# ScalarE's weight splits between the steps of a block, the last delta set's norm inside the output blocks, and the low part first in the merge, in a ten-stage float32 kernel

## The chip, the core and the metric

The kernel runs on one core of a Trainium2 chip. The metric is the time of the whole program on the device in microseconds (us). Five engines work side by side: TensorE (PE, matmuls; PEld is its weight load), VectorE (DVE), ScalarE (ACT), GpSimd (POOL) and SyncE (SP, which issues most DMAs). They meet through semaphores.

## What is computed

The reference passes one sequence of 256 tokens with 1024 features through ten residual stages, all in float32:

```python
def first_block(x, ...):                       # twice (DEPTH = 2)
    h = rms_norm(x, attn_norm[l]);  x = x + hybrid_mixer(h, ...)   # three attentions, merged
    h = rms_norm(x, ffn_norm[l]);   x = x + conv_ffn(h, ...)
# hybrid_mixer ends in
    z = g_a * (o_moba @ w_branch_moba) + g_b * (o_nsa @ w_branch_nsa) + g_c * (o_gla @ w_branch_gla)
    return z @ w_out
# conv_ffn
    a = causal_depthwise_conv(a, 3 taps) + conv_b;  return (gelu(a) * g) @ w_down
def second_block(x, ...):                      # twice
    ff = swiglu(rms_norm(h));   h = h + 0.5 * rms_norm(ff)
    mix = short_conv_mixer or gated_deltanet_mixer;  h = h + rms_norm(mix)
    ff = swiglu(rms_norm(h));   h = h + 0.5 * rms_norm(ff)
# gated_deltanet_mixer ends in
    o = o * rsqrt(mean(o * o) + eps) * norm_w        # per head, 16 heads of 128
    o = o * silu(z);  return o @ w_out
```

## The kernel before

**Stages.** In order: HYBRID, FFN1, HYBRID, FFN1, FFN2, SHORT, FFN2, FFN2, DELTA, FFN2. HYBRID is the three-branch mixer, FFN1 the convolving feed-forward layer, FFN2 the Silu-gated one, SHORT the short convolution, DELTA the gated delta rule. A stage ends in blocks, one for each tile of 128 hidden features: 22 in an FFN stage, 8 in HYBRID and SHORT, 16 in DELTA.

**Weights and their halves.** Weights come as panels of 128 x 1024 floats (512 KB), loaded by SP into a ring of six slots (`raw`). A float32 product is made of three faster ones: ScalarE writes the high part of a panel, `hi(p)` (L982 to L988: it waits until the panel has landed and the product that used the slot six panels ago is done), VectorE the low part, `lo(p)` (L1513 to L1516: raw minus high part), and TensorE takes high x high, high x low and low x high (`mm3`, L2275 to L2277). SP reloads a slot when the `lo` of its panel is done. `hi_to(p)` and `lo_to(p)` do all that is left up to panel p.

**A block f.** TensorE makes the up products (two panels of 24 matmuls of 256 columns in an FFN stage; one in HYBRID, `branches`, which takes the three branch weights) and then `down(f - 2)`: 12 matmuls of 512 columns with the hidden tile of block f - 2 as weights, added up in four banks over all blocks. In between, VectorE reads the up products (`first`, `second`), ScalarE applies Silu, or in FFN1 the middle tap (L1046) and, after VectorE's two other taps (L1652, L1655), Gelu (L1050); VectorE multiplies to `h`; ScalarE writes its high part `hhi` (L1059, which waits for `down(f - 2)`, the last user of that buffer), VectorE its low part `hlo` (`h_low`, L1676), one block later. `down(f)` needs `hlo` of f and the `lo` of its own panel. The panels of a stage lie in the order of use, and `ahead_panel(s, f)` is the last panel that block f + 1 needs (in DELTA the down panel of block f).

**Order on the engines.** Each engine's order is written by hand and is kept: an instruction that waits holds all that stands behind it. ScalarE's body of block f is: the `hi` of what block f + 1 needs, then `ffn_block(s, f)`. VectorE's is: the `lo` of what block f + 1 needs, then its own `ffn_block`. In FFN stages blocks 4 to 19 run in a hardware loop of two blocks a turn (`run_blocks`); the others are written out. In HYBRID ScalarE is one block further ahead than elsewhere. There VectorE's block is five merge steps (three products with the gates, two sums, L1617 to L1624) and then `h_low(f - 1)`.

**DELTA.** 32 tiles of q, k and v and 15 of 16 z products run in 47 slots t = 0 to 46. The delta rule is worked off in four sets of four heads, on a schedule by slot. A set's outputs are copied by ScalarE, squared and summed over each head's columns (`delta_o_squared`, eight squares, L1415), scaled and shifted by VectorE (`delta_o_added`), rooted by ScalarE (`delta_o_root`, needs a load of its function table), inverted and multiplied in by VectorE (`delta_o_inv`, `delta_o_scaled`). For the last set the squares and the sum stand in slot 46, the root behind output block 1, inverse and scaling behind block 2. An output block f: TensorE transposes head f's output (2 matmuls, L2371; it waits for `h` of f - 2, and heads 12 to 15, pairs 6 and 7, for the last set's scaling), in block 1 it also makes the sixteenth z product, and then `down(f - 2)`. VectorE makes `h` (L1667).

Of the kernel before, what the change touches and what calls it, by code (L numbers as in the profile page):

```python
# [39 lines left out]
SET = 2 * KSET  # L40
SETS = KH // KSET
# [259 lines left out]
def build(nc, stages, arrays):  # L301
# [14 lines left out]
    with ExitStack() as ctx:  # L316
# [661 lines left out]
        def _(act):  # L978
# [53 lines left out]
            def ffn_block(s, f, turn):  # L1032
# [7 lines left out]
                elif kind in (FFN2, DELTA):  # L1040
                    act.activation(act_out[:, sl, :], first[:, sl, 2:], ACT.Silu).then_inc(act_done, 1)  # L1041
                elif kind != HYBRID:

                    c = plus(convs_before(s) + f, turn, UNROLL)
                    if kind == FFN1:
                        act.activation(conv[:, sl, :], first[:, sl, 2:], ACT.Identity,  # L1046
                                       scale=tap(s, 2, f, turn), bias=conv_bias(s, f, turn)) \
                            .then_inc(tap_done, 1)
                        act.wait_ge(conv_done, c + 1)
# [9 lines left out]
                act.activation(hhi[:, sl, :], h[:, sl, :], ACT.Copy).then_inc(hhi_done, 1)  # L1059

            def blocks_of(s):
                def body(f, turn):
                    nb = n_blocks(s)
                    if turn is not None:
                        for j in range(n_up(s) + 1):
                            hi(up_panel(s, f + 1, j), turn)
                        split[0] = up_panel(s, nb - 2, n_up(s)) + 1
                    else:
                        hi_to(ahead_panel(s, f + 1 if stages[s][0] == HYBRID and 0 < f < nb - 1 else f))
                    ffn_block(s, f, turn)  # L1070
                    if f == 1 and stages[s][0] == DELTA:
                        delta_o_root(1)
                    if f == nb - 1:
                        hi_to(down_panel(s, f) + LEAD)
                run_blocks(act, s, body)
# [332 lines left out]
            def delta_o_squared(n):  # L1408

                act.wait_ge(d["o_copied"], 2 * (n + 1))  # L1410
                for i in range(SET * CHUNKS):
# [13 lines left out]
            def delta_step(s, n, o):  # L1425
# [17 lines left out]
                if p == 22:  # L1443
                    delta_o_squared(n)
# [57 lines left out]
        def _(dve):  # L1502
# [95 lines left out]
            def ffn_block(s, f, turn):  # L1598
# [13 lines left out]
                elif kind == HYBRID:  # L1612

                    dve.wait_ge(y["merged"], 3 * KT * (hybrids_before(s) + 1))
# [10 lines left out]
                    if f >= 1:  # L1625
                        h_low(s, f - 1, turn)
# [13 lines left out]
                else:  # L1640
                    dve.tensor_tensor(first[:, sl, 2:], pair[:, 0:S], rstd[:], ALU.mult).then_inc(gate_scaled, 1)  # L1641
                    dve.tensor_tensor(second[:, sl, :], pair[:, S:], rstd[:], ALU.mult).then_inc(pair_read, 1)

# [35 lines left out]
            def blocks_of(s):  # L1679
                def body(f, turn):  # L1680
                    nb = n_blocks(s)
                    if turn is not None:
                        for j in range(n_up(s) + 1):
                            lo(up_panel(s, f + 1, j), turn)
                        split[0] = up_panel(s, nb - 2, n_up(s)) + 1
                    else:
                        lo_to(ahead_panel(s, f))
                    ffn_block(s, f, turn)
                    if f == 2 and stages[s][0] == DELTA:
# [512 lines left out]
            def delta_step(s, n, o):  # L2202
# [23 lines left out]
                if p == (23 if n + 1 < SETS else 22):  # L2226
                    delta_o_added(n)
# [721 lines left out]
```

## Time and profile before

| | us |
|---|---|
| median of 3 runs | 2023.91 (2023.28 to 2025.52) |
| the profiled execution | 2025.12 |
| its span, first to last instruction | 2023.3 |
| TensorE busy | 1979.2 |
| VectorE busy | 1389.5 |
| ScalarE busy | 1105.3 |
| mean granted TensorE clock | 0.995 |

The page has the busy time of each engine; the timeline lists instructions with start, duration and, in brackets, the idle time of their engine before them with what ended it. A matmul's duration covers more than the time for which it holds the engine, so successive matmuls overlap and the distance of their starts is what counts.

### The profile page before, as it was taken

What the parts mean: (1) busy time and instruction counts of PE and PEld (TensorE: products, weight loads), DVE (VectorE), ACT (ScalarE), POOL (GpSimd) and SP (SyncE); (2) the same over time, 40 slices, a digit from 0 to 9 for tenths busy, and PEclk for the clock granted to TensorE, in tenths of its full rate; (3) what the DMA queues carried; (4) which work ended last, traced back from release to release, by engine and by line L of the source; (5) the groups of instructions that cost most, each with busy time, mean ns of one, the idle gap of its engine ahead of it and who ended that gap; (6) DMA issues with size and microseconds to landing.
All of it is one profiled execution on the core that took longest, in us unless ns stands there. A gap on an engine that the chain in (4) does not pass through costs nothing. (4 is left out here: it accounts for less than half of the span.)

```text
span 2023.3 us, 40582 instructions
## 1 busy us (share of the span) xinstructions
PE 1979.2 (98%) x15118; PEld 1841.5 (91%) x15118; DVE 1389.5 (69%) x2352; ACT 1105.3 (55%) x1836; POOL 125.4 (6%) x204
## 2 busy tenths in 40 slices
PE   8999999999999999999999999999999999999998
PEld 6999899989998999899999999999999999979997
DVE  5687877676788777765567765575559876567555
ACT  5665555566654655554454544464448786546443
POOL 2031000000130000000000000000002422000000
PEclk9999999999999999999999999999999999999999
DMA  9433655554335555465546455555555444345552
GB/s 309 146 126 126 210 193 187 191 178 146 133 119 177 178 187 187 167 208 187 188 166 212 154 195 187 187 178 187 188 178 166 134 140 149 126 146 186 187 188 93
DMA packets 117812, 348.42 MB, mean 172 GB/s; under 512 B 23288, under 2 KB 35912, under 8 KB 117184
## 3 DMA queue, kind: packets, MB, share of 16 engines
q1 hardware_dynamic: 114960, 335.23, 48.9%
q0 software_dynamic: 2736, 11.59, 1.8%
q8 instruction: 80, 1.31, 0.3%
q14 instruction: 36, 0.29, 0.0%
HBM read 340.81 MB, written 5.96 MB: 171 GB/s over the span
## 5 line engine op out<-in xcount | busy, mean ns | idle before, releaser
L1516 DVE TENSOR_TENSOR wlo<-raw,whi 128x1024 fp32r<-128x1024 f32 x621 | 737.9, 1229 | 382.6 <-ACT whi L988 381.5
L2275 PE MATMUL bank<-xhi,whi 128*128 128x256 f32 x3368 | 955.5, 284 | 9.7 <-DVE xlo L1527 5.2
L2276 PE MATMUL bank<-xlo,whi 128*128 128x256 f32 x3368 | 941.7, 280 | 0.0
L2277 PE MATMUL bank<-xhi,wlo 128*128 128x256 f32 x3368 | 941.1, 279 | 0.0
L2275 PEld LDWEIGHTS bank<-xhi,whi 128*128 128x128 f32 x3368 | 633.8, 188 | 25.2 <-issue 7.3
L2276 PEld LDWEIGHTS bank<-xlo,whi 128*128 128x128 f32 x3368 | 634.2, 188 | 5.7
L2277 PEld LDWEIGHTS bank<-xhi,wlo 128*128 128x128 f32 x3368 | 633.6, 188 | 0.0
L988 ACT ACTIVATE whi<-raw 128x1024 fp32r<-128x1024 f32 x621 | 621.2, 1047 | 6.8 <-PE bank L2277 5.3
L2275 PE MATMUL bank<-whi,hhi 128*128 128x512 f32 x688 | 273.7, 398 | 6.5 <-DVE hlo L1676 5.1
L2277 PE MATMUL bank<-whi,hlo 128*128 128x512 f32 x688 | 271.6, 395 | 0.0
L2276 PE MATMUL bank<-wlo,hhi 128*128 128x512 f32 x688 | 271.1, 394 | 0.0
L1059 ACT ACTIVATE hhi<-h 128x256 fp32r<-128x256 f32 x172 | 72.1, 419 | 266.7 <-PE bank L2277 182.6
L1041 ACT ACTIVATE act_out<-first 128x256 f32<-128x256 f32 x89 | 37.4, 420 | 230.7 <-DVE first L1641 230.3
L2275 PEld LDWEIGHTS bank<-whi,hhi 128*128 128x128 f32 x688 | 129.5, 188 | 34.8 <-issue 10.5
L2277 PEld LDWEIGHTS bank<-whi,hlo 128*128 128x128 f32 x688 | 129.8, 189 | 30.2
L2276 PEld LDWEIGHTS bank<-wlo,hhi 128*128 128x128 f32 x688 | 130.4, 190 | 23.3
L1641 DVE TENSOR_TENSOR first<-bank,rstd 128x256 f32<-128x256 f32 x132 | 55.8, 422 | 52.8 <-PE bank L2277 52.6
L1676 DVE TENSOR_TENSOR hlo<-h,hhi 128x256 fp32r<-128x256 f32 x172 | 71.8, 417 | 12.6 <-ACT hhi L1059 12.6
L1046 ACT ACTIVATE conv<-first,cols 128x256 f32<-128x256 f32 x44 | 26.5, 603 | 92.9 <-DVE first L1641 92.9
L1670 DVE TENSOR_TENSOR h<-act_out,second 128x256 f32<-128x256 f32 x132 | 55.8, 422 | 22.7 <-ACT act_out L1050 21.6
L1141 ACT ACTIVATE arena<-arena 128x256 f32<-128x256 f32 x48 | 20.0, 418 | 70.2 <-DVE arena L1791 70.2
L929 POOL DMA_DIRECT2D arena<-gains_in x6 | 3.3, 553 | 865.8 <-DVE arena L1555 734.8
(367 smaller groups left out, 1792.6 us busy)
## 6 DMA issues: line engine op xcount, KB each, us to landing
raw<-panels SPq DMA_DIRECT2D x621, 512.0 KB, 4.3
arena<-w_in POOLq DMA_DIRECT2D x2, 2048.0 KB, 10.0
arena<-relay SPq DMA_DIRECT2D x8, 512.0 KB, 4.8
arena<-gains_in POOLq DMA_DIRECT2D x6, 512.0 KB, 4.0
relay<-arena POOLq DMA_DIRECT2D x4, 512.0 KB, 8.1
relay<-arena SPq DMA_DIRECT2D x4, 512.0 KB, 4.1
x<-x_in SPq DMA_DIRECT2D x1, 1024.0 KB, 5.0
arena<-bias_table POOLq DMA_DIRECT2D x8, 128.0 KB, 4.6
```

What stands on the lines that cost most here:

```text
L988: act.activation(whi[slot][:], raw[slot][:], ACT.Copy).then_inc(hi_done, 1)
L1041: act.activation(act_out[:, sl, :], first[:, sl, 2:], ACT.Silu).then_inc(act_done, 1)
L1046: act.activation(conv[:, sl, :], first[:, sl, 2:], ACT.Identity, scale=tap(s, 2, f, turn), bias=conv_bias(s, f, turn)) \
L1059: act.activation(hhi[:, sl, :], h[:, sl, :], ACT.Copy).then_inc(hhi_done, 1)
L1141: act.activation(g, g, ACT.Tanh, scale=0.5).then_inc(y["merged"], 1)
L1516: dve.tensor_tensor(wlo[slot][:], raw[slot][:], whi[slot][:].bitcast(F32), ALU.subtract) \
L1641: dve.tensor_tensor(first[:, sl, 2:], pair[:, 0:S], rstd[:], ALU.mult).then_inc(gate_scaled, 1)
L1670: dve.tensor_tensor(h[:, sl, :], gated, second[:, sl, :], ALU.mult).then_inc(h_done, 1)
L1676: dve.tensor_tensor(hlo[:, sl, :], h[:, sl, :], hhi[:, sl, :].bitcast(F32), ALU.subtract) \
L2275: pe.matmul(dst, w_hi, a_hi, start=start, stop=False, skip_group_check=True)
L2276: pe.matmul(dst, w_hi, a_lo, start=False, stop=False, skip_group_check=True)
L2277: return pe.matmul(dst, w_lo, a_hi, start=False, stop=stop, skip_group_check=True)
```

## The change

Three edits in the order of work; no arithmetic is altered.

In FFN stages ScalarE takes the weight splits for block f + 2 (`ahead`) inside block f: one right after its Silu or tap, the rest after `hhi`. Before, they stood at the start of block f + 1's body. VectorE, in block 0 of FFN stages, does one `lo` fewer ahead of reading the first products, and that one after. In DELTA's blocks from 1 on ScalarE is one down panel further ahead. The last set's eight squares move from slot 46 to behind `hhi` of blocks 1 and 2, four each; the sum goes from slot 46 to behind VectorE's block 3, the root behind ScalarE's block 3, inverse and scaling behind VectorE's block 5. In HYBRID's blocks VectorE makes `hlo` of block f - 1 before the merge steps of f instead of after.

```diff
@@ ScalarE, ffn_block
-            def ffn_block(s, f, turn):
+            def ffn_block(s, f, turn, ahead):
...
                 elif kind in (FFN2, DELTA):
                     act.activation(act_out[:, sl, :], first[:, sl, 2:], ACT.Silu).then_inc(act_done, 1)
+                    for p in ahead[0:1]:
+                        hi(p, turn)
...
                             .then_inc(tap_done, 1)
+                        for p in ahead[0:1]:
+                            hi(p, turn)
                         act.wait_ge(conv_done, c + 1)
...
                 act.activation(hhi[:, sl, :], h[:, sl, :], ACT.Copy).then_inc(hhi_done, 1)
+                for p in ahead[1:]:
+                    hi(p, turn)
@@ ScalarE, blocks_of
                     if turn is not None:
-                        for j in range(n_up(s) + 1):
-                            hi(up_panel(s, f + 1, j), turn)
-                        split[0] = up_panel(s, nb - 2, n_up(s)) + 1
+                        ahead = [up_panel(s, f + 2, j) for j in range(n_up(s) + 1)]
+                        split[0] = up_panel(s, nb - 1, n_up(s)) + 1
+                    elif loops(s):
+                        hi_to(ahead_panel(s, f))
+                        ahead = list(range(split[0], ahead_panel(s, f + 1) + 1)) if f < nb - 1 else []
+                        split[0] += len(ahead)
                     else:
-                        hi_to(ahead_panel(s, f + 1 if stages[s][0] == HYBRID and 0 < f < nb - 1 else f))
-                    ffn_block(s, f, turn)
-                    if f == 1 and stages[s][0] == DELTA:
-                        delta_o_root(1)
+                        hi_to(ahead_panel(s, f + 1 if stages[s][0] in (HYBRID, DELTA) and 0 < f < nb - 1 else f))
+                        ahead = []
+                    ffn_block(s, f, turn, ahead)
+                    if stages[s][0] == DELTA:
+                        if f in (1, 2):
+                            delta_o_squared(SETS - 1, range(4 * f - 4, 4 * f))
+                        if f == 3:
+                            delta_o_root(1)
@@ ScalarE, delta_step
-                if p == 22:
-                    delta_o_squared(n)
+                if p == 22 and n + 1 < SETS:
+                    delta_o_squared(n, range(SET * CHUNKS))
@@ VectorE, ffn_block
                 elif kind == HYBRID:
 
+                    if f >= 1:
+                        h_low(s, f - 1, turn)
                     dve.wait_ge(y["merged"], 3 * KT * (hybrids_before(s) + 1))
...
                     dve.tensor_tensor(h[:, sl, :], second[:, sl, :], conv[:, sl, :], ALU.add).then_inc(h_done, 1)
-                    if f >= 1:
-                        h_low(s, f - 1, turn)
                     return
...
                     dve.tensor_tensor(second[:, sl, :], pair[:, S:], rstd[:], ALU.mult).then_inc(pair_read, 1)
+                    if f == 0:
+                        lo_to(ahead_panel(s, f))
@@ VectorE, blocks_of
+                    elif loops(s) and f == 0:
+
+                        lo_to(ahead_panel(s, f) - 1)
                     else:
                         lo_to(ahead_panel(s, f))
                     ffn_block(s, f, turn)
-                    if f == 2 and stages[s][0] == DELTA:
+                    if f == 3 and stages[s][0] == DELTA:
+                        delta_o_added(SETS - 1)
+                    if f == 5 and stages[s][0] == DELTA:
                         delta_o_inv(1)
                         delta_o_scaled((6, 7))
@@ VectorE, delta_step
-                if p == (23 if n + 1 < SETS else 22):
+                if p == 23 and n + 1 < SETS:
                     delta_o_added(n)
```

## Rows read from the trace of the kernel before

**Rows 1.** The page: span, busy time, the weight copy, and loads until landing.
```profile
span 2023.3 us, 40582 instructions
...
PE 1979.2 (98%) x15118; PEld 1841.5 (91%) x15118; DVE 1389.5 (69%) x2352; ACT 1105.3 (55%) x1836; POOL 125.4 (6%) x204
...
L988 ACT ACTIVATE whi<-raw 128x1024 fp32r<-128x1024 f32 x621 | 621.2, 1047 | 6.8 <-PE bank L2277 5.3
...
raw<-panels SPq DMA_DIRECT2D x621, 512.0 KB, 4.3
```

**Rows 2.** Timeline (start, us, engine, what, idle before), FFN1's loop: PE, then ACT.
```profile
332.79 0.28 PE L2275 MATMUL bank<-xhi,whi 128*128 128x256 f32 x1
...
338.39 0.39 PE L2275 MATMUL bank<-whi,hhi 128*128 128x512 f32 x1
...
341.17 0.28 PE L2275 MATMUL bank<-xhi,whi 128*128 128x256 f32 x1
...
336.24 0.42 ACT L1050 ACTIVATE act_out<-conv 128x256 f32<-128x256 f32 x1 [1.29 <-DVE conv L1655]
...
337.55 2.94 ACT L988 ACTIVATE whi<-raw 128x1024 fp32r<-128x1024 f32 x3
```

**Rows 3.** Stretches: length, busy us (count) of PE, PEld, DVE, ACT, POOL; clock, DMA.
```profile
350.00:375.00 25.00, 25.00 (x181) 23.44 (x180) 17.67 (x28) 12.97 (x18) 0.00 (x0) 1.00 0.57 189
...
1767.98:1772.40 4.42, 4.41 (x12) 3.42 (x13) 1.47 (x3) 2.86 (x4) 0.00 (x0) 0.61 0.28 106
...
1776.29:1813.59 37.30, 35.70 (x155) 27.05 (x155) 21.52 (x34) 15.05 (x22) 0.00 (x0) 1.00 0.45 155
```

**Rows 4.** Timeline, first HYBRID stage, its block 1 on DVE and down(0) on PE.
```profile
203.09 0.41 DVE L1617 SCALAR_TENSOR_TENSOR second<-arena,bank 128x256 f32<-128x256 f32 x1
...
204.88 0.42 DVE L1676 TENSOR_TENSOR hlo<-h,hhi 128x256 fp32r<-128x256 f32 x1
205.21 2.35 DVE L1516 TENSOR_TENSOR wlo<-raw,whi 128x1024 fp32r<-128x1024 f32 x2
...
205.44 0.47 PE L2275 MATMUL bank<-whi,hhi 128*128 128x512 f32 x1 [1.71 <-DVE hlo L1676]
```

**Rows 5.** Timeline, first FFN1 stage, end of DVE's block 1 and PE's block 3.
```profile
262.38 0.42 DVE L1670 TENSOR_TENSOR h<-act_out,second 128x256 f32<-128x256 f32 x1 [0.48 <-ACT act_out L1050]
264.23 3.50 DVE L1516 TENSOR_TENSOR wlo<-raw,whi 128x1024 fp32r<-128x1024 f32 x3 [1.43 <-ACT whi L988]
...
265.60 0.36 PE L2275 MATMUL bank<-xhi,whi 128*128 128x256 f32 x1 [1.03 <-DVE wlo L1516]
```

**Rows 6.** Timeline, DELTA's output blocks: PE, DVE and ACT, then the last blocks.
```profile
1761.71 0.60 PE L2371 MATMUL bank<-masks,arena 128*128 128x128 f32 x4
1762.07 0.36 PE L2275 MATMUL bank<-xhi,whi 128*128 128x256 f32 x1
...
1765.17 0.24 DVE L2181 SCALAR_TENSOR_TENSOR arena<-arena 128x4 f32<-128x4 f32 x2 [2.83 <-ACT psq L1415]
...
1766.45 0.48 DVE L1667 SCALAR_TENSOR_TENSOR h<-bank,cols,arena 128x256 f32<-128x256 f32 x1
...
1767.08 0.41 PE L2371 MATMUL bank<-masks,arena 128*128 128x128 f32 x2 [1.96 <-DVE h L1667]
...
1768.71 1.28 ACT L1423 ACT_TABLE_LOAD   x1
...
1776.58 0.42 ACT L1059 ACTIVATE hhi<-h 128x256 fp32r<-128x256 f32 x1 [2.02 <-DVE h L1667]
...
1777.98 1.23 DVE L1516 TENSOR_TENSOR wlo<-raw,whi 128x1024 fp32r<-128x1024 f32 x1 [1.44 <-ACT whi L988]
1779.12 0.42 DVE L1676 TENSOR_TENSOR hlo<-h,hhi 128x256 fp32r<-128x256 f32 x1
...
1779.68 0.47 PE L2275 MATMUL bank<-whi,hhi 128*128 128x512 f32 x1
...
1817.31 0.47 PE L2275 MATMUL bank<-whi,hhi 128*128 128x512 f32 x1 [0.69 <-DVE hlo L1676]
```

More of the change, by code:

```diff
@@ L1406, in delta_o_copied, with delta_o_squared @@
                     act.activation(o_pair(KSET * n + g), bank[g][:], ACT.Copy).then_inc(d["o_copied"], 1)
-            def delta_o_squared(n):
+            def delta_o_squared(n, parts):
                 act.wait_ge(d["o_copied"], 2 * (n + 1))
-                for i in range(SET * CHUNKS):
+                for i in parts:
                     at = SET * CHUNKS * n + i
```

## The prediction

> **What bounds the kernel now.** I read the page first: over a span of 2023.3 us TensorE is busy 1979.2 us, VectorE 69%, ScalarE 55% [rows 1]. That alone says little, because the ends of matmuls are modelled, so I looked at the starts. In the loop of an FFN stage 48 matmuls of 256 columns go from 332.79 to 338.39 (0.117 us each) and 12 of 512 columns from there to 341.17 (0.232 us each); a block is 8.38 us, without a hole [rows 2]. A stretch of such a loop is busy 25.00 of 25 us at full clock [rows 3]. Here a faster ScalarE or VectorE buys nothing. So the change can pay only where a matmul starts later than the one before it allows. I went through TensorE's timeline for such starts and asked of each what ended the wait, and then through the DELTA output blocks, whose holes are so short and regular that no row calls them idle.
>
> The true hole is the idle time that a row gives plus the overlap of the matmul before it (its duration less its spacing: 0.28 - 0.12, or 0.39 - 0.23, 0.16 us in both [rows 2]).
>
> **Part 1, the merge's low part first.** In block 2 of a HYBRID stage TensorE starts down(0) at 205.44 after 1.71 idle, so the hole is 1.87 us and TensorE was free at 203.57. It waits for hlo(0), which VectorE makes at 204.88 behind the five merge steps that began at 203.09, although hhi(0) was made in the block before [rows 4]. Moved to the front, hlo(0) runs 203.09 to 203.50 and down(0) starts at about 203.65, with the 0.14 that now lies between hlo's end (205.30) and the matmul. The five merge steps slide back by 0.33, but VectorE's sum over the block is the same, so the two lo steps still begin at 205.21, the first ending at about 206.43 (half of 2.35 us for two). TensorE, 1.79 us earlier, is done with down(0) at 203.65 + 2.78 = 206.43 and waits again for that lo, some 0.14. Behind it VectorE has nothing late: its next lo pair is one block of work on (2.35 + 2.1 = 4.4 us, so from 209.6), and wanted at 212.1. I take 1.65 us per stage, bounds 1.3 and 1.8; the other HYBRID stage has the same hole (its row, not shown, says 1.71 idle as well). Sum 3.3 us. The new order queues hlo(f-1)'s wait for hhi ahead of the merges; hhi(f-1) is ScalarE's first act after h(f-1), before its weight copies, so nothing is held.
>
> **Part 2, weight copies between steps, FFN stages.** The body of block f+1 followed at once on that of block f, so three hi copies already ran right behind hhi(f). What moves is one of them, to between the tap (or Silu) of f and hhi(f). In the loop ScalarE idles 1.29 us there, waiting for VectorE's convolution before the Gelu [rows 2]; a copy takes 1.05 [rows 1], and 0.95 when one follows another (2.94 for three) [rows 2]. It fits, at no cost, and the two behind hhi end 0.95 sooner. If the cover were gone, each block would put about 1 us on a cycle of ScalarE and VectorE that the copies leave 1 us shorter: zero again. In the loop this is worth nothing, for TensorE has no hole. Worth something is the start of FFN1: at 265.60 TensorE waits for the first lo of a group of three that began at 264.23 after ScalarE's copies; idle 1.03, hole 1.2 [rows 5]. After the change that panel's hi is made right after the tap of block 1, some 3 us before VectorE asks for it, so VectorE can begin this lo once it has made h (262.80, [rows 5]) instead of at 264.23, 1.4 us earlier, and block 0 gains another half microsecond because only two lo's stand before its scaling. TensorE is free at 264.40, the lo would end near 262.8 to 264.0: the hole goes, 1.2 us, bounds 0.9 and 1.2, twice (the second FFN1 stage has the like, idle 1.04). Sum 2.4 us. The four FFN2 stages' starts show no wait for wlo, I cost them at nothing.
>
> **Part 3, the last DELTA set's norm, and the copies one block ahead.** Four holes stand in the output blocks [rows 6].
> (a) Before block 2's transposes TensorE idles 1.96, hole 2.12: h(0) is made at 1766.45, behind a lo, behind VectorE's wait of 2.83 us for ScalarE's eight squares. down(0) follows at 1768.0 [rows 3]. Without squares and sum in front, VectorE does that lo straight after its read of the last z product, which TensorE had finished by 1761.71, so at about 1762.3 to 1763.5; h(0) ends at 1763.9, hhi(0) at 1764.4, hlo(0) at 1764.8. TensorE ends the last up product at 1767.08 - 2.12 = 1764.96, transposes, and starts down(0) at about 1765.2: 2.8 us, bounds 2.6 and 2.8.
> (b) down(0) itself runs at a granted clock of 0.61, between the levels 1.2 and 2.4 GHz [rows 3]: 4.42 us instead of 2.78, right behind that idle time; 1.6 us, if the clock stays as full as it is behind this stretch; bounds 0 and 1.6.
> (c) Then downs that start 3.39 us apart (37.30 us for eleven from 1776.29 to 1813.59 [rows 3]). They are not TensorE's: VectorE waits 1.44 us in each for a hi, ScalarE 2.02 for h. The cycle is hi 1.05, lo 1.15, hlo 0.33, h 0.48, hhi 0.32 with short waits between, and hlo's end releases TensorE. With hi one panel ahead VectorE's share is lo, hlo, h = 2.0 us and ScalarE's hhi, hi = 1.4; the cycle is cut, TensorE's own work sets the pace: 12 x 0.232 = 2.78 and two transposes. Transposes that wait for nothing take 0.36 for four (1761.71 to 1762.07), so 0.18 for two; the blocks now show 0.52. I take 3.04 us a block, bounds 2.96 and 3.15. From down(1) to down(13) there are 12 intervals, and the restart ahead of down(1) is shorter too, by 0.3: 12 x 0.35 + 0.3 = 4.5 us, bounds 3.0 and 5.4. The load of a panel, 4.3 us to landing [rows 1], is issued six panels ahead, some 18 us.
> (d) Before down(14), at 1817.31, TensorE idles 0.69, hole 0.85: hlo(14) stands behind a lo that waited for its hi. With hi and lo early this goes: 0.8 us, bounds 0.6 and 0.9.
> What is moved in: squares of 1.2 us on ScalarE in each of blocks 1 and 2, a root with table load of 1.5 us in block 3, sum and 1.5 us of inverse and scaling on VectorE in blocks 3 and 5. ScalarE has 3.04 - 1.3 = 1.7 us free in a block and VectorE 1.0, and both run one to two blocks ahead of TensorE; the scaled pairs are wanted in block 12. I cost them at 0, bounds 0 and 0.8 loss. Sum 2.8 + 1.6 + 4.5 + 0.8 = 9.7.
>
> A rule weighed here: before the root the row shows a load of 1.28 us at 1768.71 and the root at once behind it, with no further pause [rows 6]. The Trainium skill, "ScalarE: Activation LUTs", section "What ACT_TABLE_LOAD costs", adds a drain of about 1.4 us to each switch. By that figure ScalarE would lose 2.9 instead of 1.5 us in block 3, still inside its lead; the sum is the same.
>
> **Sum.** 3.3 + 2.4 + 9.7 = 15.4 us. Made against the profiled execution, 2023.3 span and 2025.1 in all, it gives 2009.7 [rows 1]; this execution lies 1.2 above the median of the three runs (2023.9), so the time I give is 2023.9 - 15.4 = 2008.5. The bounds of the parts add to 9.8 to 16.7 us, so 2007.2 to 2014.1, and the runs of before spread over 2.2 us.
>
> **Rivals.**
> A. The DELTA blocks stay near 3.39 us, because something else paces them: for instance TensorE's restart behind the two transposes (0.52 now, though no row of it names a wait). For it: the first matmul after them is stretched (0.47 against 0.40). Against it: hlo ends just 0.14 before each restart (1779.54, 1779.68 [rows 6]) and both engines wait on each other with no slack. Gain 15.4 - 4.5 = 10.9, 2013.0.
> B. The clock falls elsewhere or still falls in down(0), with 1.6 to 2 us lost: 2010.3. For it: such drops stand where TensorE has idled. Against it: 12 blocks each with a pause ran at 1.00 [rows 3].
> C. Slower. The moved copy waits in ScalarE's queue for its panel, and Gelu, hhi and all copies wait behind it, where before hhi went first. The load of a panel of block f+2 is issued when the lo of block f is done, before TensorE's 332.79 [rows 2]; it is now asked for at the tap's end, which is 336.24 - 1.29 + 8.38 = 343.3 in the next block, so landing must take over 10.5 us against a median of 4.3 [rows 1]. If it took half a microsecond more than that, each of 132 FFN blocks could pay up to it: 132 x 0.5 = 66, 2074.
> D. Nothing changes: ScalarE's order was not what held VectorE, and each hole returns behind the next wait (for the lo of down(1), for hhi behind the end of the last down): within 4 us, about 2022. The releasers named in the rows speak against it in all five places.
>
> **Chances.** Forecast 0.70, A 0.13, B 0.09, C 0.03, D 0.05. What a measurement can tell from no change is 0.2%, 4 us. Faster 0.92, the same 0.05, slower 0.03. The range takes in the bounds, A and B and half the spread of runs: 2005.5 to 2014.5.
>
> **What would show it.** After: no idle before down(0) of the HYBRID stages over 0.3 us; no wait for wlo in block 3 of FFN1; block 2's transposes of DELTA directly behind the last up product, full clock in down(0), starts of downs 3.0 to 3.1 us apart, no ACT row with an idle of 2.02 for h; FFN loops still 8.38 us. Wrong I would be if downs stand 3.3 or more apart, if a wait for hhi or for a landed panel appears in their place, or if a FFN loop's block grows.

## The result, and the profile after

The changed kernel takes 2004.03 us (median of 4 runs, 2003.44 to 2004.42). The kernel before, run beside it on the same chip, takes 2024.59 us (2023.28 to 2025.52). The ratio is 0.9899, with a 95% interval of 0.9882 to 0.9916: 20.6 us faster, where 15.4 was forecast. The time lies 1.5 us below the range. The sign and most of the sum were right, and something of about 5 us was missing from it.

The page of the changed kernel (span; busy time; groups of instructions with busy time, mean ns of one, and idle time of the engine before them; a load's median until landing) stands against [rows 1]:

```profile
span 2002.0 us, 40567 instructions
...
PE 1970.4 (98%) x15118; PEld 1838.6 (92%) x15118; DVE 1401.1 (70%) x2352; ACT 1100.3 (55%) x1836; POOL 125.7 (6%) x204
...
L1529 DVE TENSOR_TENSOR wlo<-raw,whi 128x1024 fp32r<-128x1024 f32 x621 | 749.6, 1230 | 218.1 <-ACT whi L988 215.1
...
L988 ACT ACTIVATE whi<-raw 128x1024 fp32r<-128x1024 f32 x621 | 632.3, 1045 | 7.0 <-PE bank L2297 5.5
L2295 PE MATMUL bank<-whi,hhi 128*128 128x512 f32 x688 | 272.7, 396 | 0.0
...
raw<-panels SPq DMA_DIRECT2D x621, 512.0 KB, 3.6
```

The span is 21.3 us shorter. No engine does less: the copies and low parts have the counts of before, and TensorE's busy time fell by 8.8 us only. What went is waiting. Down projections have no idle time ahead of them (0.0), and VectorE waits 215 us for ScalarE's weight copies. In the kernel before, the same two groups read:

```profile
L1516 DVE TENSOR_TENSOR wlo<-raw,whi 128x1024 fp32r<-128x1024 f32 x621 | 737.9, 1229 | 382.6 <-ACT whi L988 381.5
...
L2275 PE MATMUL bank<-whi,hhi 128*128 128x512 f32 x688 | 273.7, 398 | 6.5 <-DVE hlo L1676 5.1
```

A fall of 166 us in VectorE's wait and a gain of 21: most of that wait never reached TensorE. To find where the 21 us came from I took the start of each matmul in both timelines (both kernels issue the same 15118 in the same order) and read how the difference, after less before, moves along the run:

| stretch, by the time in the kernel before | difference at its start and end | gained | forecast |
|---|---|---|---|
| HYBRID 1, to 212.0 | +0.06, -1.60 | 1.7 | 1.65 |
| start of FFN1 stage 1, 240 to 280 | -1.60, -3.07 | 1.5 | 1.2 |
| **end of FFN1 stage 1, 400 to 450** | -3.07, -4.62 | 1.5 | **0** |
| HYBRID 2, to 628 | -4.62, -6.29 | 1.7 | 1.65 |
| start of FFN1 stage 2, 670 to 690 | -6.32, -7.78 | 1.5 | 1.2 |
| **end of FFN1 stage 2, 840 to 870** | -7.78, -9.32 | 1.5 | **0** |
| up to the middle of DELTA, 870 to 1570 | -9.32, -9.39 | 0.1 | 0 |
| **middle of DELTA, 1570 to 1592** | -9.39, -10.79 | 1.4 | **0** |
| DELTA output blocks, 1760 to 1830 | -10.78, -21.31 | 10.5 | 9.7 |

Timeline, first HYBRID stage of the changed kernel (start, us, engine, what), against [rows 4]:

```profile
203.13 0.42 DVE L1691 TENSOR_TENSOR hlo<-h,hhi 128x256 fp32r<-128x256 f32 x1
...
203.69 0.47 PE L2295 MATMUL bank<-whi,hhi 128*128 128x512 f32 x1
...
205.25 2.35 DVE L1529 TENSOR_TENSOR wlo<-raw,whi 128x1024 fp32r<-128x1024 f32 x2
...
206.62 0.36 PE L2295 MATMUL bank<-xhi,whi 128*128 128x256 f32 x1
```

hlo runs first, and down(0) starts at 203.69 (forecast 203.65), 1.81 us earlier. Some 0.15 of it is given back ahead of the up product at 206.62, which follows 0.28 behind a matmul instead of 0.23 and has a longer duration: the pause for the lo pair at 205.25.

Timeline, first FFN1 stage, VectorE's block 1 and TensorE's block 3, against [rows 5]:

```profile
259.79 1.22 DVE L1529 TENSOR_TENSOR wlo<-raw,whi 128x1024 fp32r<-128x1024 f32 x1
261.31 2.36 DVE L1529 TENSOR_TENSOR wlo<-raw,whi 128x1024 fp32r<-128x1024 f32 x2 [0.30 <-ACT whi L988]
...
262.63 0.28 PE L2295 MATMUL bank<-xhi,whi 128*128 128x256 f32 x1
```

The lo that TensorE used to wait for is made right behind h, and TensorE goes on at 262.63 without an idle time.

Timeline, DELTA's output blocks, against [rows 6]; below it two stretches (length, busy us and count of PE, PEld, DVE, ACT, POOL, granted clock, DMA share, GB/s), against [rows 3]:

```profile
1754.18 0.38 PE L2391 MATMUL bank<-masks,arena 128*128 128x128 f32 x2
1754.31 0.47 PE L2295 MATMUL bank<-whi,hhi 128*128 128x512 f32 x1
...
1760.89 1.28 ACT L1436 ACT_TABLE_LOAD   x1
1762.18 0.21 ACT L1436 ACTIVATE arena<-arena 128x8 f32<-128x8 f32 x1
...
1766.35 0.48 PE L2295 MATMUL bank<-whi,hhi 128*128 128x512 f32 x1
...
1769.37 0.48 PE L2295 MATMUL bank<-whi,hhi 128*128 128x512 f32 x1
...
1772.49 0.42 ACT L1063 ACTIVATE hhi<-h 128x256 fp32r<-128x256 f32 x1 [1.63 <-PE bank L2297]
1772.94 0.43 DVE L1691 TENSOR_TENSOR hlo<-h,hhi 128x256 fp32r<-128x256 f32 x1 [0.82 <-ACT hhi L1063]
```

```profile
350.00:375.00 25.00, 25.00 (x181) 23.44 (x180) 17.90 (x28) 12.86 (x18) 0.00 (x0) 1.00 0.53 185
...
1754.31:1757.31 3.00, 3.00 (x17) 2.43 (x16) 2.35 (x5) 2.65 (x11) 0.00 (x0) 1.00 0.51 178
```

The transposes follow the last up product, down(0) runs at a granted clock of 1.00, downs start 3.02 us apart in the two rows (1766.35, 1769.37) and 3.01 in the mean, and ScalarE's hhi waits for the end of a down product on TensorE, no longer for h. VectorE waits 0.82 us for hhi, which the prediction had named as a sign of being wrong, but TensorE has no idle row in any of these blocks: it sets the pace here now. The FFN loop is what it was, busy 25.00 of 25 us.

### The profile page after: what moved, and what is told of

Its sections match the earlier page's. It is cut to its first block, busy times and chain, and to the rows that moved or that the text cites. A ratio compares the mean times of both kernels' runs of the same rounds, so it can differ in the third digit from the quotient of the medians.

```text
span 2002.0 us, 40567 instructions
## 1 busy us (share of the span) xinstructions
PE 1970.4 (98%) x15118; PEld 1838.6 (92%) x15118; DVE 1401.1 (70%) x2352; ACT 1100.3 (55%) x1836; POOL 125.7 (6%) x204
## 4 chain that ended last, share of the span: by engine, by line
PE 90%; DVE 4%; ACT 3%; issue 1%; DMA 1%; POOL 1%; SPq 0%; DVEq 0%; ACTq 0%; POOLq 0%
PE bank L2295 28%; PE bank L2296 27%; PE bank L2297 27%; PE bank L2774 1%; ACT whi L988 1%; PE bank L2585 1%; DVE wlo L1529 1%; DVE arena L1568 1%; PE bank L2329 1%; PE bank L2558 0%; DVE conv L2030 0%; PE bank L2546 0%; PE bank L2338 0%; DVE xlo L1540 0%; DMA relay<-arena 0%
## 5 line engine op out<-in xcount | busy, mean ns | idle before, releaser
L1529 DVE TENSOR_TENSOR wlo<-raw,whi 128x1024 fp32r<-128x1024 f32 x621 | 749.6, 1230 | 218.1 <-ACT whi L988 215.1
L988 ACT ACTIVATE whi<-raw 128x1024 fp32r<-128x1024 f32 x621 | 632.3, 1045 | 7.0 <-PE bank L2297 5.5
```

Source lines behind the costliest of these rows:

```text
L988: act.activation(whi[slot][:], raw[slot][:], ACT.Copy).then_inc(hi_done, 1)
L1529: dve.tensor_tensor(wlo[slot][:], raw[slot][:], whi[slot][:].bitcast(F32), ALU.subtract) \
```

## The experiments

"Before" is the kernel before, run beside each on the same chip (medians 2025.15 to 2025.66); shifts are differences of matmul starts, as in the table above, from one profile of each kernel. The medians also take in differences in stretches that no edit touches, as in the middle of DELTA below: e4 gains 7.9 us by its median and 5.9 by the shifts where its edit acts, e5 2.2 and 3.1. So what a part is worth is read from the shifts. Line numbers differ a little from kernel to kernel.

### The parts, each alone

**e1**: the merge's low part first, nothing else.

```diff
                 elif kind == HYBRID:
+                    if f >= 1:
+                        h_low(s, f - 1, turn)
...
                     dve.tensor_tensor(h[:, sl, :], second[:, sl, :], conv[:, sl, :], ALU.add).then_inc(h_done, 1)
-                    if f >= 1:
-                        h_low(s, f - 1, turn)
```

> The kernel before with the low part first in the merge and nothing else. Theory (separate holes): both HYBRID stages lose 1.65 us, 3.3 in all, and the first FFN1 stage still has its wait for wlo of 1.2 us at its block 3 and for x of 1.2 us behind its last product. Rival (the parts help each other, the change is worth more than its parts): under 2 us alone. Rival (the merge part frees VectorE for the whole stage): over 5 us.

Measured: 2021.88 us against 2025.47, 0.9983 (0.9974 to 0.9993). The HYBRID stages gain 1.67 and 1.68 us, 3.35 together, and starts and ends of FFN1 stand as they were.

**e2**: all of the DELTA hunks and nothing else (copies one block ahead, the squares in blocks 1 and 2, root in 3, sum in 3, scaling in 5).

```diff
-                        hi_to(ahead_panel(s, f + 1 if stages[s][0] == HYBRID and 0 < f < nb - 1 else f))
+                        hi_to(ahead_panel(s, f + 1 if stages[s][0] in (HYBRID, DELTA) and 0 < f < nb - 1 else f))
...
+                        if f in (1, 2):
+                            delta_o_squared(SETS - 1, range(4 * f - 4, 4 * f))
+                        if f == 3:
+                            delta_o_root(1)
```

> The kernel before with both edits of DELTA's output blocks (copies one panel further ahead, norm of the last set moved) and nothing else. Theory: 10.5 us faster, starts of successive downs 3.02 us apart, down(0) at full clock. Rival (the granted clock in the middle of DELTA depends on the change): 11.5 to 12 us, with one spell of low clock less there in every run; if that spell is chance, the run lands at 10.5 or at 11.8 according to its own trace.

Measured: 2014.75 against 2025.47, 0.9949 (0.9932 to 0.9966). Output blocks: 10.7 us.

**e3**: all of the FFN hunks and nothing else (`ahead` between tap or Silu and hhi, in start, loop and end; block 0's lo moved).

```diff
+                        for p in ahead[0:1]:
+                            hi(p, turn)
                         act.wait_ge(conv_done, c + 1)
...
+                for p in ahead[1:]:
+                    hi(p, turn)
```

> The kernel before with the edits of the FFN stages alone (copies between the steps, one lo after the first read). Theory (lag): 2 x (1.2 to 1.3 at the start + 1.5 to 1.6 at the end of FFN1) = 5.6 us faster; the wait for x behind the last product of FFN1 is gone. My prediction had only the start: 2.4 us.

Measured: 2018.41 against 2025.47, 0.9968 (0.9958 to 0.9978). Each FFN1 stage gains 1.4 us at its start and 1.55 at its end. The gains of e1, e2 and e3 by medians (3.6, 10.7, 7.1) add to 21.4, against 20.6 for the whole change. By the shifts where the edits act they are 3.35, 10.7 and 5.9, 19.95 in all, against 19.9 in the whole change (21.3 less the 1.4 in the middle of DELTA): the three parts are independent. So the end of FFN1 was what the forecast lacked, and it comes from the FFN edit.

### Why does an edit of copies help the end of FFN1?

In the kernel before, the last matmuls of a FFN1 stage and VectorE's work beside them read so:

```profile
424.01 0.42 DVE L1641 TENSOR_TENSOR first<-bank,rstd 128x256 f32<-128x256 f32 x1
...
428.55 2.36 DVE L1516 TENSOR_TENSOR wlo<-raw,whi 128x1024 fp32r<-128x1024 f32 x2 [0.52 <-ACT whi L988]
430.83 2.48 DVE L1579 TENSOR_TENSOR x<-x,bank 128x512 f32<-128x512 f32 x4
...
432.25 1.93 PE L2318 MATMUL bank<-masks,x 128*128 128x128 f32 x13 [1.04 <-DVE x L1579]
```

and in the changed kernel:

```profile
419.39 0.42 DVE L1654 TENSOR_TENSOR first<-bank,rstd 128x256 f32<-128x256 f32 x1 [2.56 <-PE bank L2297]
...
423.94 2.36 DVE L1529 TENSOR_TENSOR wlo<-raw,whi 128x1024 fp32r<-128x1024 f32 x2 [0.52 <-ACT whi L988]
426.22 2.47 DVE L1592 TENSOR_TENSOR x<-x,bank 128x512 f32<-128x512 f32 x4
...
427.64 2.26 PE L2338 MATMUL bank<-masks,x 128*128 128x128 f32 x16
```

The transposes of x at the stage's end wait for VectorE's update of x, which stands behind two lo's, behind h, behind the last block's first read. That hole makes 1.1 of the 1.55; the other 0.4 are short pauses before the last two downs (425.24 and 428.17 in the kernel before), each 0.14 behind the end of an hlo that is as late. Before, VectorE reached that first read without an idle time, so it was late. After, it had waited 2.56 us for TensorE. One theory was that the copies between steps in the loop make each block's cycle shorter and so work the delay off. The rival was that the delay is made once, at the stage's start, and only carried. Three kernels part them.

**e4**: copies between steps in blocks 0 to 2 only, with block 0's lo moved; loop and end as before (the line is shown against the changed kernel's; the loop has the order of before).

```diff
-                        ahead = list(range(split[0], ahead_panel(s, f + 1) + 1)) if f < nb - 1 else []
+                        ahead = list(range(split[0], ahead_panel(s, f + 1) + 1)) if f < 3 else []
```

> As the FFN edits alone, but only in blocks 0, 1 and 2; the loop and the end are those of before. Theory L (the lag of VectorE behind TensorE that the start leaves is carried through the loop, since the cycle of ScalarE and VectorE there is as long as TensorE's block, and shows at the end): the start's hole goes and the lag in the loop shrinks by 1 to 2 us, so that the end's hole shrinks too, 4.5 to 5.6 us in all. Rival E (the end's hole is made by the order of the last two blocks alone): 2.4 to 2.6 us, hole at the end as before, 1.1 us each.

Measured: 2017.57 against 2025.47, 0.9963 (0.9949 to 0.9977). Starts 1.4 and 1.4, ends 1.57 and 1.54: all that e3 gives, with the loop of before.

**e5**: the opposite, block 3, the loop and block 20 without the start, lo not moved.

```diff
+                        ahead = list(range(split[0], ahead_panel(s, f + 1) + 1)) if f == 3 or nb - 2 <= f < nb - 1 else []
```

> The kernel before with copies between the steps in the loop and the last two blocks of the FFN stages, blocks 0 to 2 as before. Theory L: the holes at the start stay (1.2 us in each FFN1 stage), the cycle of ScalarE and VectorE is 1 us shorter in the loop, so VectorE's lag of 3.8 us behind the up products is gone after some four or five turns and the end's hole with it: 2 x 1.5 = 3.0 us faster. If the start's hole is also the cause of the end's hole directly: no gain.

Measured: 2022.92 against 2025.16, 0.9988 (0.9979 to 0.9998). Starts 0, ends 1.57 and 1.54.

**e6**: block 20, the last but one, alone; loop as before.

```diff
+                        ahead = list(range(split[0], ahead_panel(s, f + 1) + 1)) if nb - 2 <= f < nb - 1 else []
```

> As before, with a copy between the steps only in block 20, the last but one, of the FFN stages. Theory L: the lag in the loop stays at 3.8 to 3.4 us; in the last block VectorE's first read comes 1.0 us earlier (one copy less stands behind hhi), so the end's hole shrinks by about 1 us: 2 x 1.0 = 2 us faster, starts unchanged. If the lag of the loop fixes the end whatever stands there: no gain.

Measured: 2022.40 against 2025.16, 0.9988 (0.9979 to 0.9998). Starts 0, ends 1.19 and 1.25; what is left is the row at 430.62 below.

Each closes the hole at the end, e6 nearly, so it has more than one remedy. How each does it is seen in the middle of the loop. Each pair is TensorE's start of down, which is where the up products are done, and VectorE's first read of them: before (its down start is 338.39, [rows 2]), after, e4, e5. The row behind these is the end of the stage in e6.

```profile
342.04 0.42 DVE L1641 TENSOR_TENSOR first<-bank,rstd 128x256 f32<-128x256 f32 x1
```

```profile
343.71 0.39 PE L2295 MATMUL bank<-whi,hhi 128*128 128x512 f32 x1
343.92 0.42 DVE L1654 TENSOR_TENSOR first<-bank,rstd 128x256 f32<-128x256 f32 x1 [1.13 <-PE bank L2297]
```

```profile
345.12 0.39 PE L2292 MATMUL bank<-whi,hhi 128*128 128x512 f32 x1
346.59 0.42 DVE L1653 TENSOR_TENSOR first<-bank,rstd 128x256 f32<-128x256 f32 x1
```

```profile
346.43 0.39 PE L2285 MATMUL bank<-whi,hhi 128*128 128x512 f32 x1
346.63 0.42 DVE L1651 TENSOR_TENSOR first<-bank,rstd 128x256 f32<-128x256 f32 x1 [1.13 <-PE bank L2287]
```

```profile
430.62 2.26 PE L2330 MATMUL bank<-masks,x 128*128 128x128 f32 x16 [0.30 <-DVE x L1591]
```

VectorE's lag behind TensorE is 3.65 us before, 0.21 after, 1.47 in e4 and 0.20 in e5. Followed over blocks 2 to 21 of the stage, the lag goes

- before: 6.03, 4.31, 3.87, 3.82, ... 3.39, 3.31, 1.75;
- after: 3.74, 2.17, 0.59, 0.20, and 0.20 to the end;
- e4: 3.74, 2.15, 1.70, 1.64, ... 1.17, 1.07, 0.20;
- e5: 6.03, 4.31, 2.72, 1.54, 0.31, 0.20, and 0.20 to the end.

Before, the lag falls by some 0.03 us a block (3.82 in block 5, 3.39 in block 19): the cycle of ScalarE and VectorE takes that much less than TensorE's block of 8.38. Made in the first two blocks, it is still there 20 blocks later, and nothing shows it in between, because TensorE has its weights in time all the way. It comes due where the stage ends and TensorE wants x itself. Both theories hold a part: the start makes the lag and curing it there is enough (e4); the loop with copies between steps has more slack and works it off in three blocks (e5). Done together they don't add. Over both stages e4 gives 2.8 us at the starts and 3.1 at the ends, e5 gives the same 3.1 at the ends, and e3, which has both, gives 5.9.

**e11 and e12** split e4: only block 0's lo behind the first reads, and only the copies of the first blocks.

```diff
+                    if f == 0:
+                        lo_to(ahead_panel(s, f))
```

> The kernel before with VectorE's lo moved behind the first read in block 0 of FFN stages and nothing else. Theory: reads come 1.1 us earlier, but Gelu's table load sits behind the tap, so h gains 0.5 to 1 us; the hole at block 3 shrinks by as much and so does the end's: 2 x (0.5 to 1.0) x 2 holes = 2 to 4 us faster.

> The kernel before with the copies between the steps in blocks 0, 1 and 2 of the FFN stages, without the move of the lo. Theory: hi of block 3's first panel is ready early, so its lo follows h directly: 1.4 us at block 3, enough for the hole of 1.2; lag in the loop 1.6 to 2.2 us instead of 3.8; the end's hole almost gone: 2 x (1.2 + 1.0 to 1.5) = 4.4 to 5.4 us faster.

Measured: e11 2023.15 against 2025.66, 0.9992 (0.9982 to 1.0001): starts 0.67 and 0.71, ends nothing, 1.4 us in all, where its expectation had 2 to 4. Its lag is 5.52 in block 2, but from block 3 on it is that of before (4.30, 3.86): the lo move takes half a microsecond off one block, and the next wait takes it back. e12 2020.33, 0.9974 (0.9964 to 0.9984): starts 1.43 and 1.48, ends 1.12 and 1.07. The copies alone do the whole of the start, and lo and copies together the whole of the end.

**e9**: the changed kernel with two copies between tap and Gelu, to see how deep the cover is.

```diff
                             .then_inc(tap_done, 1)
-                        for p in ahead[0:1]:
+                        for p in ahead[0:2]:
                             hi(p, turn)
...
-                for p in ahead[1:]:
+                for p in ahead[2 if kind == FFN1 else 1:]:
```

> The changed kernel with two copies instead of one between FFN1's tap and its Gelu. The idle time there is 1.2 us, two copies take 2.0, so Gelu, h and hhi come 0.8 us later in each of 44 blocks and one copy less stands behind hhi. Theory (TensorE alone sets the pace of the loop; VectorE has lost its lag and waits for it): the same time as the changed kernel, FFN block 8.39 us. Rival (the room is used up and each block pays): 44 x 0.8 = 35 us slower.

Measured: 2004.85 against 2025.66, 0.9899 (0.9883 to 0.9916). Each start and end gains within 0.13 us of what it does in the changed kernel, and the loop's blocks are the same. VectorE's lag goes 4.42, 3.09, 1.71, 0.50, 0.20: worked off one block later. ScalarE has the room for a second copy, but it pays nothing.

### The DELTA blocks: are the two edits one?

**e7**: only the copies one block ahead. **e8**: only the norm moved into the blocks. Each is its share of e2's diff, the first hunk (`in (HYBRID, DELTA)`) and the rest.

> The kernel before with ScalarE one down panel further ahead in DELTA's blocks, the norm of the last set left in slot 46. Theory: starts of downs 3.02 us apart, last hole gone: 4.5 + 0.8 + 0.2 = 5.5 us faster, the idle time of 2.12 before block 2 and the low clock in down(0) stay. Rival: the copy of down(3) now stands ahead of hhi(2) and behind the root's table load, so hlo(1) or hlo(2) comes late: 4 us.

> The kernel before with only the norm of the last set moved into blocks 1 to 5. Theory: the idle time before block 2 (2.8 us to the start of down(0)) and the low clock (1.6 us) go: 4.4 us. Against it stands that the squares and the root lengthen a cycle that has no slack: 1.2 us in each of blocks 1 and 2, 1.5 in block 3: at worst 3.9 us back, so between 0.5 and 4.4 us faster. Together with the other edit this must give 10.1 to 10.5.

Measured: e7 2018.40 against 2025.16, 0.9965 (0.9953 to 0.9976), output blocks 6.1 us. e8 2024.93, 0.9994 (0.9984 to 1.0004), output blocks 0.8 us. The interval of e8 takes in 1, so only its shift tells. Together (e2) they give 10.7, so 3.8 us belong to neither alone. e8's timeline gives one reason: down(1) to down(4) on PE, then the lo's on DVE between them:

```profile
1770.52 0.47 PE L2280 MATMUL bank<-whi,hhi 128*128 128x512 f32 x1 [1.14 <-DVE hlo L1679]
1775.08 0.47 PE L2280 MATMUL bank<-whi,hhi 128*128 128x512 f32 x1 [1.32 <-DVE hlo L1679]
1779.98 0.47 PE L2280 MATMUL bank<-whi,hhi 128*128 128x512 f32 x1 [1.66 <-DVE hlo L1679]
1783.37 0.47 PE L2280 MATMUL bank<-whi,hhi 128*128 128x512 f32 x1 [0.15 <-DVE hlo L1679]
...
1773.37 1.22 DVE L1519 TENSOR_TENSOR wlo<-raw,whi 128x1024 fp32r<-128x1024 f32 x1 [2.60 <-ACT whi L988]
1778.28 1.23 DVE L1519 TENSOR_TENSOR wlo<-raw,whi 128x1024 fp32r<-128x1024 f32 x1 [2.81 <-ACT whi L988]
1781.66 1.23 DVE L1519 TENSOR_TENSOR wlo<-raw,whi 128x1024 fp32r<-128x1024 f32 x1 [1.43 <-ACT whi L988]
```

At down(1) e8 has gained 3.4 us. Then the squares (1.17 us on ScalarE, from 1771.12) and the root with its load (1.40 us, from 1775.80) stand in ScalarE's queue ahead of the copy that VectorE waits for (2.60 and 2.81 us, against 1.43 without them), in a cycle without slack. The next three intervals are 4.56, 4.90 and 3.39 us: 1.17 and 1.51 over the third, so 2.7 us are given back. In the changed kernel the same squares and root lie in the same blocks, and the downs are 3.01 apart. e7 shows the other side:

```profile
1768.03 0.41 PE L2371 MATMUL bank<-masks,arena 128*128 128x128 f32 x2 [1.96 <-DVE h L1667]
1768.94 0.47 PE L2275 MATMUL bank<-whi,hhi 128*128 128x512 f32 x1 [0.50 <-DVE hlo L1676]
```

The entry is as in [rows 6], with its idle time and a down(0) of 4.4 us, and behind it blocks of 3.01 in the mean. Here the low clock costs time: down(0) to down(1) takes 4.56 us, and hlo(1) had been ready for 2.6. In the kernel before it cost nothing. Whether the clock falls behind the same 1.96 us of idle time is not set by the code here: of the nine kernels that keep this entry, it fell in three (before, e4, e7) and stayed full in six (e1, e3, e5, e6, e11, e12). This is down(1) in the kernel before, then down(0) as a stretch and down(1) in e1, which has DELTA's code of before:

```profile
1772.90 0.48 PE L2275 MATMUL bank<-whi,hhi 128*128 128x512 f32 x1
```

```profile
1762.46:1765.24 2.78, 2.77 (x12) 2.30 (x13) 0.26 (x1) 2.46 (x4) 0.00 (x0) 1.00 0.41 167
```

```profile
1767.38 0.47 PE L2275 MATMUL bank<-whi,hhi 128*128 128x512 f32 x1 [1.68 <-DVE hlo L1676]
```

At a full clock down(0) takes 2.78 us instead of 4.42, and TensorE then waits 1.68 for hlo(1): from down(0) to down(1) it is 4.91 us in both, and in the other five kernels too. hlo(1) sets the start of down(1), and it comes earlier only with the copies ahead: down(1) gains 0.5 more than down(0) in e8, 1.9 in e2. So of the 3.8 us, some 1.56 (4.56 less 3.00) are the low clock that e7's profile happened to have, and the rest is the 2.7 that e8 gives back, less the 0.5 that both edits bring at down(1).

### The middle of DELTA: 1.4 us that no edit made

At 1583.44 of the kernel before, TensorE has idled 3 us for a transfer; the changed kernel has the same wait, untouched by any hunk. The timeline's row with its idle time, and the stretch of 7 us from there (columns as above), before:

```profile
1583.44 2.89 PE L2754 MATMUL bank<-arena 128*128 128x128 f32 x16 [3.14 <-DMA arena<-relay]
```

```profile
1583.44:1590.44 7.00, 6.50 (x34) 6.45 (x35) 5.30 (x13) 4.38 (x8) 0.00 (x0) 0.57 1.03 350
```

after:

```profile
1573.95 2.29 PE L2774 MATMUL bank<-arena 128*128 128x128 f32 x9 [3.04 <-DMA arena<-relay]
```

```profile
1573.95:1580.95 7.00, 6.26 (x42) 6.20 (x43) 6.06 (x14) 4.48 (x8) 0.00 (x0) 0.79 1.04 347
```

The granted clock of the same work behind the same idle time was 0.57 before and 0.79 after. These are means: the clock is at 1.00 or 0.50 (2.4 or 1.2 GHz), and the mean tells for how much of the stretch it was low. If the change does that, it should repeat; if chance does, another run of the same kernel shows another value; and if TensorE's idle time is the cause, matmuls put there should keep the clock at 1.00. **e15** is the changed kernel again. **e13** puts 13 matmuls of 512 columns in the wait, into a PSUM bank that nobody reads then (added work whose result is overwritten), **e14** 6 of them. **e10**, earlier, put 12 ahead of the wait for the transfer but behind another.

```diff
             def delta_w16(n):
+                if n == 0:
+                    pe.wait_ge(d["exponent"], 2 * KSET)
+                    pe.wait_ge(d["eg"], 2 * KSET)
+                    for _ in range(13):
+                        pe.matmul(bank[7][:], xhi[:, 0, 0:P], xhi[:, 0:2, :].rearrange("p a b -> p (a b)"),
+                                  start=True, stop=True, skip_group_check=True)
                 pe.wait_ge(d["tri_in"], 16 * (n + 1))
```

> The changed kernel with 12 matmuls of 512 columns, 2.8 us, whose result is overwritten, put where TensorE waits 3.2 us in the middle of DELTA for a DMA (before the first set's inverse is used). Theory (the spell of low clock right behind that wait follows from TensorE's idling, and costs 1.4 us for each of its two lengths): the spell is gone and the kernel 0.5 to 2 us faster, its runs closer together. Rival (the spell comes whatever TensorE did): same time or up to 1 us slower.

> The changed kernel with 13 matmuls of 512 columns (3.0 us, result overwritten) that start at once where TensorE waits 3.2 us in the middle of DELTA for a DMA. Theory (TensorE's idling brings the spell of low clock, which in the traces so far lasts 3.4, 6.8 or 10.2 us and costs 1.7, 2.6 or more): no spell there, 1.7 us or more faster than the changed kernel beside it. Rival (the spell comes from what follows, the small products of the inverse, which leave the engine little to do): the spell is there as before, same time.

> The same with 6 matmuls, 1.4 us, so that a hole of 1.8 us stays. Theory: no spell or a shorter one, 0 to 1.7 us faster than the changed kernel. Rival as above: same time as the changed kernel.

> The changed kernel itself, on the same chip as the two with the filled hole. Its spell in the middle of DELTA lasts 3.4, 6.8 or 10.2 us by chance; the gain against the kernel before on this chip is 20.5 to 21.5 us, and the mean of the middle spell is no shorter than before the change.

Measured: e10 2004.37 against 2025.66, 0.9898 (0.9881 to 0.9915). Its matmuls waited too: they start at 1573.14, after 2.17 us of idle time put down to ScalarE, so this kernel says nothing on the question. Then, on one chip with before at 2025.15: e13 2003.24 (2002.94 to 2003.77), e14 2004.28 (2003.58 to 2005.12), e15 2005.38 (2004.68 to 2006.73); as ratios 0.9894 (0.9877 to 0.9910), 0.9897 (0.9880 to 0.9913) and 0.9904 (0.9887 to 0.9920). The stretch behind the wait in e15, then e13's timeline row and its stretch:

```profile
1574.01:1581.01 7.00, 7.00 (x33) 7.00 (x34) 5.14 (x12) 4.25 (x8) 0.00 (x0) 0.50 1.02 345
```

```profile
1574.68 0.49 PE L2774 MATMUL bank<-arena 128*128 128x128 f32 x2 [0.83 <-DMA arena<-relay]
```

```profile
1574.68:1581.68 7.00, 5.62 (x49) 5.56 (x50) 5.98 (x12) 3.75 (x6) 0.00 (x0) 1.00 1.03 355
```

The same kernel ran this stretch at 0.79 once and at 0.50 once, which refutes that the change sets it. The other profiles agree: in fourteen kernels and repeats that leave this wait unfilled (3.0 to 3.4 us idle), the 7 us behind it ran at 0.50 to 0.86, and the clock fell in all of them. Against the kernel before, the work of 1570 to 1592 took from 1.4 us less (after, e1, e3, e4, e5) to 1.2 us more (e12), and none of these kernels edits it.

With the wait filled the stretch ran at 1.00, though the same small products follow; it is one profile against fourteen. e13 is 2.1 us faster than e15 beside it (2.14 in the medians), and the two spreads don't touch. That is four runs each on one chip. The changed kernel's first runs, taken at another time, go down to 2003.44 and overlap with e13's (up to 2003.77); in the one that was profiled the clock was low for only a part of the stretch (0.79), and e13's transfer landed 0.7 us later (1574.68 for 1573.95), so by 1592 the two are level. The 2.1 us are a gain over long spells of low clock, not over every run. e15 itself gained 19.8 us over the kernel before on its chip, where 20.5 to 21.5 were expected.

Behind half the fill the clock still fell: e14's granted clock is 0.99 from 1570 to 1580 and 0.84 from 1580 to 1590, where the changed kernel has 0.83 and 1.00. That the fill put the fall off is not shown, for e2, e7 and e11 have no fill, and there the clock falls nearly as late (5.0 us behind the wait, 5.6 in e14).

e13 is the fastest kernel of this study.

## Why the prediction was right, and where it was wrong

**Part 1** came out as worked: down(0) at 203.69 for 203.65, 3.3 us for 3.3, the small pause behind it included.

**Part 2, start.** 2.9 us for 2.4. The hole of 1.2 went, and two things around it were not counted: the first matmul behind a hole is 0.08 us slow in its spacing (0.36 long at 265.60 in [rows 5], 0.28 at 262.63 after), and blocks 1 and 2 had pauses of 0.1 in all, too short to be called idle.

**Part 2, end: the step that failed.** It is the sentence "In the loop this is worth nothing, for TensorE has no hole". The first half is right, e4 shows that the loop's copies give nothing of their own. The conclusion was wrong, because it took the state of TensorE for the state of the kernel. VectorE ran 3.65 us behind in mid-loop and 3.31 at its end; that could have been read from VectorE's rows, in which no first read of this stage waits for TensorE. The sum then left the hole at 432.25, with its releaser "DVE x L1579", at nothing, although I had asked of every hole what ended it: I stopped at the releaser and did not ask what had made it late. Following it back (x, two lo's, hlo, h, first read) leads to the first blocks, which the change edits. It was put at 0 and measured 3.1 us of 21.3, the largest error; with it the forecast would have been 2005.4.

**Part 3.** 10.5 for 9.7. (a) 2.9 for 2.8. (b) with the restart ahead of down(1) 1.9 for 1.9 (1.6 for the clock, 0.3 for the restart), but this is luck: the second step that failed. The low clock that it was to win back ("4.42 us instead of 2.78") cost nothing in the kernel before, since down(1) starts 4.91 us behind down(0) at a full clock as well (e1 and five others), held by hlo(1). What gave the 1.9 is that hlo(1) comes earlier with the copies ahead; without them the same place gives 0.5 (e8), and of this the sum had only the 0.3. (c) downs 3.01 apart for 3.04: 4.5 for 12 intervals, where the sum had 4.2. (d) 0.95 for 0.8, the restart again. Behind the last down another 0.24 came that the forecast did not have. The cost of the moved squares and root was put at 0 and was 0, but the reason given ("both run one to two blocks ahead") holds only together with the copies ahead; e8 shows 2.7 us when they are not. The root itself is 0.01 us behind its load's end (1760.89 + 1.28, 1762.18), so the pause that the Trainium skill adds to a switch ("ScalarE: Activation LUTs", "What ACT_TABLE_LOAD costs") is not in these rows either.

**Rivals.** A fell: downs are 3.01 apart, and what looked like a slow restart was the wait for hlo. B did not come about for down(0), where a fall would cost 1.56 us with the copies ahead (e7); the clock did change elsewhere, in the middle of DELTA, and in the other direction, by chance. C fell: the copies' idle time is 7.0 us in all, 5.5 of it for TensorE, as in [rows 1] (6.8, 5.3), and a load landed in 3.6 us. D fell in all places.

**The range** was too narrow below. Its low end took in no term for a hole that I held untouched (3.1 us) and none for the clock's own scatter (1.4 us in this pair of profiles), only half the spread of runs.

## What to carry to other kernels

An engine off the critical path can be late for a whole loop without a trace on the engine that sets the pace; read its lag (its first read behind the end of what it reads) at the loop's start and end, and price an edit of a stage's start at the stage's end too. A slow stretch costs nothing where the next step waits for another engine anyway: before a low clock is priced, look whether TensorE sets the pace there, and whether another run of the same code shows the same clock. Work moved into a cycle without slack costs its full length, and nothing once that cycle is cut, so two edits may be worth more together, or less, than the sum of the two alone. Behind a releaser that you mean to leave alone, go back one step more.

## What the runs showed of the hardware

The granted clock behind one and the same wait is not fixed. Behind the wait of about 3 us in the middle of DELTA it was 0.50 to 0.86 in fourteen profiles, 0.79 and 0.50 in two of the changed kernel, each over 7 us that begin with the restart. Behind a wait of 1.96 us in DELTA's output blocks it fell in three profiles of nine. What a fall costs depends on who sets the pace: nothing in the kernel before, where down(1) waits for hlo(1) anyway, and 1.56 us in e7, where it does not.

Between e15 (0.50) and e13 (1.00) lie 2.1 us of median, more than one start or one end of FFN1 gave. With thirteen matmuls of no use in that wait the clock stayed at 1.00 in the one profile taken, and four runs were 2.1 us faster in the median than four of e15; behind six the clock still fell. How long or how dense such a fill has to be was not tried beyond these two.
